# Attention's heads in pairs, and the division by the softmax's sums inside the turn (blocks of weights times diagonals of reciprocal sums)

## What is computed

```python
k = rope(kv[:, :, 0], pos); v = kv[:, :, 1]
q = rope((rmsnorm(x, w['attn_norm']) @ w['w_q']).reshape(b, t, 16, 64), pos)
# swa_prompt: blocks of 128 queries, keys of their own and the previous block
s = jnp.einsum('bnqkgd,bnskd->bnkgqs', qb, kb) * 64 ** -0.5
s = jnp.where(mask, s, -jnp.inf)
m = jnp.maximum(jnp.max(s, axis=-1, keepdims=True), sink)
p = jnp.exp(s - m)
p = p / (jnp.sum(p, axis=-1, keepdims=True) + jnp.exp(sink - m))
o = jnp.einsum('bnkgqs,bnskd->bqkgd', p, vb)
x = x + o @ w['w_o']
```

## Time and profile before

| | |
|---|---|
| median of 3 runs | 3170.84 us (3169.39 to 3171.84) |
| the profiled execution, its own time | 3175.33 us |
| its span in the profile | 3173.5 us |
| PE busy | 3063.0 us (97%) |
| DVE busy | 2544.1 us (80%) |
| mean granted TensorE clock | 0.979 |

### The profile page before, as it was taken

The page is one execution under the profiler, slowest core; times in us unless marked ns, Lnnn a source line. Parts: engine busy times, 40 slices in busy tenths (PEclk is TensorE's granted clock), DMA queues, the critical chain, the costliest instruction groups (busy, mean ns, idle before and its releaser), DMA issues.

```text
span 3173.5 us, 50434 instructions
## 1 busy us (share of the span) xinstructions
PE 3063.0 (97%) x19070; PEld 2973.1 (94%) x19070; DVE 2544.1 (80%) x4947; ACT 1379.8 (43%) x2558; POOL 1882.1 (59%) x1165
## 2 busy tenths in 40 slices
PE   8889999999999999999988899999999999999998
PEld 7779999999999999999875789999999999999998
DVE  7755999977776899989567448999877759998997
ACT  2522344477774333333344233343677753333333
POOL 4543488887776665664130233788877766565651
PEclk9999999999999999999987899999999999999999
DMA  3212499999999999999130022899999999999994
GB/s 111 73 54 92 139 335 347 325 403 393 394 386 367 401 401 398 400 395 398 58 99 1 27 67 85 283 348 347 355 400 394 387 360 398 401 398 400 400 397 191
DMA packets 286337, 920.89 MB, mean 290 GB/s; under 512 B 27344, under 2 KB 77136, under 8 KB 282432
## 3 DMA queue, kind: packets, MB, share of 16 engines
q1 hardware_dynamic: 154080, 415.37, 35.9%
q0 software_dynamic: 111280, 404.77, 33.3%
q10 hardware_dynamic: 20736, 97.53, 7.6%
HBM read 817.07 MB, written 102.38 MB: 290 GB/s over the span
## 4 chain that ended last, share of the span: by engine, by line
PE 67%; DVE 21%; DMA 8%; issue 2%; POOL 1%; ACT 1%; SPq 1%; DVEq 0%; ACTq 0%
PE ps L1767 24%; PE ps L1709 15%; PE ps L1632 10%; PE ps L1712 7%; DMA sring<-s_dram 6%; PE ps L1743 5%; DVE xrest L1168 2%; DVE xl L975 1%; DVE xn L982 1%; DMA gt<-gate_dram 1%; DVE low L1336 1%; DVE cand L1251 1%; DVE cand L1258 1%; DVE rowsB L1161 1%; PE ps L1893 1%
## 5 line engine op out<-in xcount | busy, mean ns | idle before, releaser
L787 ACT ACTIVATE high<-raw 128x1024 fp32r<-128x1024 f32 x512 | 542.8, 1060 | 937.2 <-PE ps L1767 640.2
L629 POOL TENSOR_TENSOR low<-raw,high 128x1024 fp32r<-128x1024 f32 x256 | 614.8, 2402 | 157.6 <-ACT high L787 154.2
L1709 PE MATMUL ps<-xh,high 128*128 128x384 f32 x2048 | 701.4, 342 | 6.3 <-ACT sring L840 6.3
L1767 PE MATMUL ps<-hh,high 128*128 128x384 f32 (+1 forms) x2048 | 691.4, 338 | 7.6 <-DVE low L1336 7.4
L1767 PE MATMUL ps<-hl,high 128*128 128x384 f32 x2048 | 691.7, 338 | 0.0
L1767 PE MATMUL ps<-hh,low 128*128 128x384 f32 x2048 | 690.7, 337 | 0.0
L1709 PE MATMUL ps<-xl,high 128*128 128x384 f32 x2048 | 688.6, 336 | 0.0
L620 POOL DMA_INDIRECT rowsB<-v,pick x192 | 330.0, 1719 | 207.1 <-DVE xrest L1168 192.3
L620 POOL DMA_INDIRECT rowsA<-v,pick x192 | 315.1, 1641 | 213.8 <-DVE xrest L1168 206.5
L1712 PE MATMUL ps<-xh,low 128*128 128x384 f32 x2048 | 399.5, 336 | 7.2 <-POOL low L629 7.2
L1767 PEld LDWEIGHTS ps<-hh,high 128*128 128x128 f32 x2048 | 385.2, 188 | 11.6 <-DVE low L1336 11.4
(11 more groups left out here) (282 smaller groups left out, 5205.3 us busy)
## 6 DMA issues: line engine op xcount, KB each, us to landing
raw<-uT SPq DMA_DIRECT2D x256, 512.0 KB, 6.8
raw<-v SPq DMA_DIRECT2D x256, 512.0 KB, 14.0
gate_dram<-gblk ACTq DMA_DIRECT2D x24, 2048.0 KB, 11.6
s_dram<-sring ACTq DMA_DIRECT2D x120, 384.0 KB, 6.8
gt<-gate_dram SPq DMA_DIRECT2D x30, 1536.0 KB, 20.9
sring<-s_dram SPq DMA_DIRECT2D x120, 384.0 KB, 14.7
raw<-wts SPq DMA_DIRECT2D x74, 512.0 KB, 3.3
rowsB<-u,pick POOLq DMA_INDIRECT x192, 8.0
```

Of the source, the lines that this page charges most:

```text
L629: pool.tensor_tensor(low[:, m % 4], raw[:, m % 4], high[:, (m + 2) % 3].bitcast(F32), ALU.subtract).then_inc(sem("lo_ready"), 1)
L787: act.activation(high[:, (m + 2) % 3], tile_raw(m), ACT.Copy).then_inc(sem("hi_ready"), 1)
L1709: pe.matmul(ps[:, m % 2, 0:DN], a[:, c], x[:, c, 0:DN], start=(c == 0 and k == 0), stop=False)
L1767: ins = pe.matmul(ps[:, c, 0:cols], w[:, c], h[:, n % 3, 0:cols], start=opens, stop=(n == KEYS - 1 and j == 2))
```

## The change

Heads are kept in pairs: `qR` has 128 partitions and 8 slots, a tile of the projection as it is, and `kR` holds each key head twice, in the lower and in the upper 64 partitions. Scores of the even head use rows 0 to 63 of the array and those of the odd head rows 64 to 127; they go to different banks. Mix writes even heads to PSUM partitions 0 to 63 and odd heads to 64 to 127, in twice as many matmuls of half the columns, and keep is one copy of 128 partitions. The division is no longer done on `pr`: DVE multiplies the identity by the reciprocal sums of the four heads (`diag`, 128 x 512), and the turn is a full fp32 matmul of a block of `pr` with a diagonal in place of a transpose. The order of heads in a unit's small arrays becomes even heads first, hence `pairs` and the rearranged sinks. The copy of the sample queries (`qS`) is made in two halves and stands behind the first two units' scale_max. PE's wait for all rotated tiles at the start becomes a wait for the tiles that a unit needs.

```diff
-        qR = st.take("qR", [HD, NH, T])
-        kR = st.take("kR", [HD, NKV, T])
+        qR = st.take("qR", [P, NC, T])
+        kR = st.take("kR", [P, NKV, T])
+        diag = st.take("diag", [P, 2, GRP, P])
@@ rope
-                    chain.did(dve.tensor_tensor(dst[:, 2 * f], rc[0:HD, r], rot[0:HD, r], ALU.add))
-                    ins = dve.tensor_tensor(dst[:, 2 * f + 1], rc[HD:P, r], rot[HD:P, r], ALU.add)
+                    if d0 == D_K:
+                        for e in range(2):
+                            rows = slice(e * HD, (e + 1) * HD)
+                            for at in range(2):
+                                ins = dve.tensor_tensor(kR[at * HD:(at + 1) * HD, 2 * f + e], rc[rows, r], rot[rows, r],
+                                                        ALU.add)
+                                if (e, at) != (1, 1):
+                                    chain.did(ins)
+                    else:
+                        ins = dve.tensor_tensor(qR[:, f], rc[:, r], rot[:, r], ALU.add)
@@ attention, DVE
-                dve.wait_ge(sem("roped"), 2 + NC)
-                dve.tensor_copy(qS[:, :, :, :], qR[:, :, TP:T].rearrange("p h (b s) -> p b h s", b=NB)
-                                ).then_inc(sem("qS_ready"), 1)
@@ normalise
-                    dve.tensor_tensor(p, p, m[:, 5, 0:GRP].unsqueeze(2).broadcast_to([P, GRP, 2 * WIN]),
+                    if u >= 2:
+                        dve.wait_ge(sem("pturn"), u - 1)
+                    dve.tensor_tensor(diag[:, u % 2], ident.unsqueeze(1).broadcast_to([P, GRP, P]),
+                                      m[:, 5, 0:GRP].unsqueeze(2).broadcast_to([P, GRP, P]),
                                       ALU.mult).then_inc(sem("p_ready"), 1)
@@ keep
-                    for e in range(2):
-                        ins = dve.tensor_copy(
-                            ob[e * HD:(e + 1) * HD, 2 * kv:2 * kv + 2, n * WIN:(n + 1) * WIN],
-                            ps[0:HD, OUT, :].rearrange("p (g e q) -> p g e q", g=2, e=2)[:, :, e])
+                    dve.tensor_copy(ob[:, 2 * kv:2 * kv + 2, n * WIN:(n + 1) * WIN],
+                                    ps[:, OUT, 0:2 * WIN].rearrange("p (g q) -> p g q", g=2)
+                                    ).then_inc(sem("o_copied"), 1)
@@ behind the first two scale_max
+                dve.wait_ge(sem("roped"), 2 + NC)
+                by_half = qS[:, :, :, :].rearrange("p b (f e) s -> p b f e s", e=2)
+                for e in range(2):
+                    ins = dve.tensor_copy(by_half[:, :, :, e], qR[e * HD:(e + 1) * HD, :, TP:T]
+                                          .rearrange("p f (b s) -> p b f s", b=NB))
@@ scores, PE
-                pe.wait_ge(sem("roped"), 2 + NC)
-                    for g in range(GRP):
-                        ins = pe.matmul(sbank(k)[:, g // 2, (g % 2) * 256 + lo:(g % 2 + 1) * 256],
-                                        qR[:, kv * GRP + g, n * WIN:(n + 1) * WIN],
-                                        kR[:, kv, ks:(n + 1) * WIN], start=True, stop=True)
+                    if u < NKV:
+                        pe.wait_ge(sem("roped"), 2 + (NC - 1 if u < NKV - 1 else NC))
+                    for g in range(2):
+                        for e in range(2):
+                            ins = pe.matmul(sbank(k)[:, e, g * 256 + lo:(g + 1) * 256],
+                                            qR[e * HD:(e + 1) * HD, 2 * kv + g, n * WIN:(n + 1) * WIN],
+                                            kR[e * HD:(e + 1) * HD, kv, ks:(n + 1) * WIN], start=True, stop=True)
@@ turn
-                            ins = pe.transpose(ps[:, 2 + kb, g * P:(g + 1) * P],
-                                               pr[:, u % PRS, g, kb * WIN:(kb + 1) * WIN], ident)
+                            ins = pe.matmul(ps[:, 2 + kb, g * P:(g + 1) * P],
+                                            pr[:, u % PRS, g, kb * WIN:(kb + 1) * WIN], diag[:, u % 2, g],
+                                            start=True, stop=True)
@@ mix
-                        ins = pe.matmul(ps[0:HD, OUT, :], vtok[:, n - 1 + kb, kv * HD:(kv + 1) * HD],
-                                        prT[:, u % 2, 4 * kb:4 * kb + 4].rearrange("p g q -> p (g q)"),
-                                        start=(kb == kbs[0]), stop=(kb == 1))
+                        for e in range(2):
+                            j = 4 * kb + 2 * e
+                            ins = pe.matmul(ps[e * HD:(e + 1) * HD, OUT, 0:2 * WIN],
+                                            vtok[:, n - 1 + kb, kv * HD:(kv + 1) * HD],
+                                            prT[:, u % 2, j:j + 2].rearrange("p g q -> p (g q)"),
+                                            start=(kb == kbs[0]), stop=(kb == 1))
```

More of the change, by code:

```diff
@@ L524, in _ @@
             spq.wait_ge(sem("k_ready"), 2)
-            spq.dma_start(kNew, kR[:, :, TP - WIN:T]).then_inc(sem("out_done"), 16)
+            spq.dma_start(kNew, kR[0:HD, :, TP - WIN:T]).then_inc(sem("out_done"), 16)
             load_weights(W_Q + 2, W_O + 2)
@@ L1400, in experts, with rope @@
                 dve.memset(mark[:, :], 0.0).then_inc(sem("x_ready"), 1)
-            def rope(d0, n, dst):
+            def rope(d0, n):
                 for f in range(n):
@@ L1419, in attention @@
                 norm_apply(N_KV, X_KV)
-                rope(D_K, 2, kR)
+                rope(D_K, 2)
                 dve.wait_ge(sem("roped"), 2)
@@ L1426, in attention @@
                 norm_apply(N_AT, X_AT, inv=rinv[:, :])
-                rope(D_Q, NC, qR)
-                dve.wait_ge(sem("roped"), 2 + NC)
-                dve.tensor_copy(qS[:, :, :, :], qR[:, :, TP:T].rearrange("p h (b s) -> p b h s", b=NB)
-                                ).then_inc(sem("qS_ready"), 1)
+                rope(D_Q, NC)
                 ob = xn
@@ L1451, in scale_max, with pairs @@
                     chain.settle()
-                    sk = prm[:, P_SINK + kv * GRP:P_SINK + (kv + 1) * GRP]
-                    chain.did(dve.tensor_tensor(m[:, 0, 0:GRP], m[:, 0, 0:GRP], sk, ALU.max))
+                    sk = prm[:, P_SINK + kv * GRP:P_SINK + (kv + 1) * GRP].rearrange("p (g e) -> p e g", e=2)
+                    def pairs(i):
+                        return m[:, i, 0:GRP].rearrange("p (e g) -> p e g", e=2)
+                    chain.did(dve.tensor_tensor(pairs(0), pairs(0), sk, ALU.max))
                     chain.settle()
@@ L1456, in scale_max @@
                     chain.settle()
-                    dve.tensor_tensor(m[:, 3, 0:GRP], sk, m[:, 0, 0:GRP], ALU.subtract
-                                      ).then_inc(sem("pmax"), 1)
+                    dve.tensor_tensor(pairs(3), sk, pairs(0), ALU.subtract).then_inc(sem("pmax"), 1)
                 def normalise(u):
-                    p, m = pr[:, u % PRS], sm[:, u % PRS]
+                    m = sm[:, u % PRS]
                     dve.wait_ge(sem("pexp"), u + 1)
@@ L1472, in keep @@
                     dve.wait_ge(sem("p_out"), u + 1)
-                    for e in range(2):
-                        ins = dve.tensor_copy(
-                            ob[e * HD:(e + 1) * HD, 2 * kv:2 * kv + 2, n * WIN:(n + 1) * WIN],
-                            ps[0:HD, OUT, :].rearrange("p (g e q) -> p g e q", g=2, e=2)[:, :, e])
-                        if e == 0:
-                            chain.did(ins)
-                    ins.then_inc(sem("o_copied"), 1)
+                    dve.tensor_copy(ob[:, 2 * kv:2 * kv + 2, n * WIN:(n + 1) * WIN],
+                                    ps[:, OUT, 0:2 * WIN].rearrange("p (g q) -> p g q", g=2)
+                                    ).then_inc(sem("o_copied"), 1)
                 def sample_scale(k, h):
@@ L1534, in attention @@
                     item(k)
+                dve.wait_ge(sem("roped"), 2 + NC)
[3 more added lines that the diff above has]
+                                          .rearrange("p f (b s) -> p b f s", b=NB))
+                    if e == 0:
+                        chain.did(ins)
+                ins.then_inc(sem("qS_ready"), 1)
                 for u in range(UNITS):
@@ L1860, in sample_scores @@
                             pe.matmul(o[:, 0:WIN], q, kc_sb[:, b, kv], start=True, stop=True)
-                            ins = pe.matmul(o[:, WIN:], q, kR[:, kv, TP + b * TS:TP + (b + 1) * TS],
+                            ins = pe.matmul(o[:, WIN:], q, kR[0:HD, kv, TP + b * TS:TP + (b + 1) * TS],
                                             start=True, stop=True)
```

## The result

The changed kernel takes 3138.28 us (median of 4 runs, 3135.36 to 3144.23), the one before 3171.34 us beside it (3169.39 to 3178.40). The ratio is 0.9894, with a 95% interval of 0.9873 to 0.9915: 33 us, 1.1%, faster. The forecast was 3148, that is 23 us off the median before. Against those the gain is 27 to 29 us.

A forecast was written before the change was run, and what follows sets the result against it. PE bounds the whole kernel; in this stage DVE's work plus its waits for PE do. DVE's 84.0 us plus waits of 8.1, 11.6, 2 and 5.1 gave 110.8, 27 saved from 3175.3: 3148 us, range 3138 to 3163.

The forecast's parts named there:

- step with a sample piece: PE in units 8 to 15: turn, mix, sample piece and scores together fall from 6.49 to 5.7 us.
- row pairs apart: Rival on PE's scores: row pairs don't overlap, costing 13 us, total 3161 us; chance 12%.
- neither pair overlapping: Rival on PE's mix and scores: switching between full and split array use drains it, total 3179 us; chance 5%.
- a turn at the price of four transposes: Rival on PE's turn: 2.2 us more in 15 steps, total 3181 us; chance 3%.
- DVE's wait for mix: Sign in the units' stage, ahead of keep: the wait should fall from 23.2 us to under 12.
- DVE without waits for PE: DVE's own work in the stage: 98.9 us, less 15.7 saved, plus 0.8 for the sample queries' copies, gives 84.0.
- Waits for PE: DVE's waits in the stage: 8.1 us PE-bound steps, 11.6 slow turns, about 2 late start, 5.1 at the end.
- Slow turns: Half-clock turn and mix, at the first turn and behind three samples' pauses: four at 2.9 us, 11.6 in all.
- PE-bound steps and the pause in unit 12: Units 8 to 15: seven steps, 8.1 us over DVE's; PE's late start behind the samples' copies, about 2 us.
- The end: Behind the last normalise: turn, mix, sample piece and last mix, less the cover of one keep, 5.1 us.
- turn and mix just fit: Units 0 to 7: turn, mix and two handovers fit beside scale_max's 3.0 us, costing nothing at full clock.
- the clock never falls once the units run: Rival on PE's clock in the units' stage: 11.6 us more are won, total 3137 us; chance 7%.

The follow-up runs named there:

- e7: The changed kernel with mix unpaired, one matmul of 512 columns a key block, and keep as two copies: 3150.70 us, ratio 0.9941 to the kernel before.
- e8: The changed kernel with all four heads' scores on rows 0 to 63, so its output is not the reference's: 3154.06 us, ratio 0.9951 to the kernel before.
- e9_change: The changed kernel itself, run again unaltered in a later series: 3138.26 us, ratio 0.9913 to the kernel before.
- e3_scores_in_row: The changed kernel with a unit's four scores ordered even, even, odd, odd: 3138.24 us, ratio 0.9919 to the kernel before.
- e6_warm_less: The changed kernel with 2, 3 and 3 extra 512-column matmuls into an unused bank ahead of turns 0, 3 and 5: 3134.43 us, ratio 0.9899 to the kernel before.

## Why the forecast was right in direction and too small

**The mechanism stood.** The terms of PE: turn 1.98 (forecast 1.9), mix 0.92 (0.95), scores 1.06 (1.05), step with a sample piece 5.74 (5.7). Those of DVE: `diag` 0.69 (0.69), one copy 0.42 (0.42), `qS` 0.86 (0.8), start 2.7 to 3.1 us earlier (3.0). Row pairs, for which I had no row, overlap as column strips do: the step with the weakest ground held. Three rivals are settled (row pairs apart, neither pair overlapping, a turn at the price of four transposes): e7 and e8 show what unpaired takes, and the turn took 1.94 times the transposes, at half clock 3.7 us against 1.9. Of the signs that the prediction named, one didn't come: DVE's wait for mix fell to 14.6 us and not under 12, mainly because of the end of the stage (below). The Trainium skill (page "TensorE: Matmul & The Clock Gate", section "Terms") has the transpose mode as four times faster for FP32; no run here shows a factor of four.

**The stage.** Forecast 116.8 us (1641.8 to 1758.6), measured 112.9. DVE without waits for PE: 84.0 forecast; 1753.9 - 1646.9 - 24.6 = 82.4 measured. Waits for PE: 26.8 forecast, 24.6 measured, but with other parts. The term of the sum that was mis-sized most is the first:

- Slow turns: 11.6 forecast (four at 2.9). There were three, none behind the samples' copies, and DVE waited 0.8, 1.95 + 0.3 and 2.8 us behind them, 5.9 in all:

```profile
1678.54 0.42 DVE L1483 COPY xn<-ps 128x256 f32<-128x256 f32 x1 [1.95 <-PE ps L1912]
...
1693.42 0.42 DVE L1483 COPY xn<-ps 128x256 f32<-128x256 f32 x1 [2.80 <-PE ps L1912]
```

- PE-bound steps and the pause in unit 12: 10.1 forecast. DVE's waits there are 1.3 four times and 1.9 once, 7.2. I had counted seven steps at 5.7; the last two have no scores left and take 4.68.

```profile
1712.31 1.23 DVE L1449 SCALAR_TENSOR_TENSOR pr<-ps,atc 128x1024 f32<-128x1024 f32 x1 [1.31 <-PE ps L1863]
```

- The end: 5.1 forecast, 3.25 + 3.24 + 2.27 = 8.8 measured (the rows of the end above), since without scores DVE has nothing to do in those two steps. Some 2.9 us of small waits stand in units 2 to 8, where the prediction had turn and mix just fit and put nothing.

**The step that failed** is the one from the sum to the number: "since part of my gain is clock, I don't take the 27 off the median (3144) but keep 3148". It took the 27.2 us off one execution of 3175.33 us, which lay 4.5 us over the median of three, and 8.6 over that of the 53 later runs. Its guess at the reason holds over the whole span: that execution's mean granted clock was 0.979, and of the 53 runs the four at 0.979 or less averaged 3175 us, the twelve at 0.983 3166.9. But most of the excess was not in this stage. What lies ahead of the first matmul of the values, and what lies behind the mark, is the same in all these kernels but for addresses. In the trace of before these parts take 1566.8 and 1387.6 us; in the 13 other traces 1557.5 to 1567.9 (mean 1563.2) and 1380.7 to 1388.4 (mean 1385.1). So some 6 us of excess stand outside the stage, and about 2.5 of the 8.6 are left for it; both are estimates, from one trace of the kernel before. How far such code varies, by the per-line view of two of the kernels (e9_change, e3_scores_in_row):

```profile
L1848 PE MATMUL ps<-wv_sb,xn x80: 378/379/430, 1561.2 to 1578.4; 128*128 128x256 f32 x64, 128*64 128x256 f32 x16
```

```profile
L1848 PE MATMUL ps<-wv_sb,xn x80: 378/379/430, 1557.5 to 1574.6; 128*128 128x256 f32 x64, 128*64 128x256 f32 x16
```

Taking 27.2 off the median would have given 3143.6, and the stage's measured 31.2 gives 3139.6; the median says 3138.3. Of the 9.7 us that I missed, 4.5 are this step, 4 the stage, and the rest lies within the runs' spread. Part of the 4 may be the same thing again: off the later median of 3166.8 the 27.2 give 3139.6, 1.3 over what was measured. The rival "the clock never falls once the units run" came nearest in its number, 3137, though not in its reason, which makes that luck: the clock did fall three times, and each fall cost less.

**What the change is made of.** The pairs and what comes with them (one copy for keep, the start) carry it all; the start's share was not run by itself and is read from the traces. The other half, the diagonals, gives nothing alone (ratio 1.0006). Beside the pairs it costs the stage 4.7 us without the filling (112.9 against 108.3) and 2.2 with it (109.4 against 107.2), one trace each; the totals (0.9894 and 0.9913 against 0.9906) can't show a difference. I had priced both sides of it nearly right, 0.54 us off DVE and 0.88 onto PE (0.96 measured), but summed the change as one and never asked what each half was worth; the sum of PE's step (5.7 against DVE's 4.53) already said that in units 8 to 12 the second half buys time on the engine that waits.

What stays open: how the 14.6 us divide between mix and the second copy of keep, and what decides whether a slow stretch follows unit 12. Even and odd heads' scores in the same bank were not tried.

## What to carry to other kernels

Where two matmuls use half the array each, in rows or in columns, put them on different halves: here PE then took 0.92 us in place of 1.77 and 1.06 in place of 1.92, and in both orders of the calls that were tried. Before work is moved from one engine to another, look in each stage which of the two waits, and cost each half of a change for itself. And take a forecast made from one profiled execution off as a difference from the median; its distance to the median belongs to the whole span unless a stage can be shown to hold it. A median of three or four runs moves too: that of the kernel before lay between 3163.8 and 3171.3 us in five series.

## What was not expected of the hardware

- PE takes matmuls of the other half of the array past several records that stand ahead of them in program order: even, even, odd, odd took 1.14 us for eight records of 256 columns, as even, odd, even, odd did.
- Row halves (64 of 128 rows) overlap nearly as fully as column halves: 1.92 to 1.06 us for scores, 1.77 to 0.92 for mix.
- A full fp32 matmul in place of a fp32 transpose takes 1.94 times as long (1.98 against 1.02 us for eight), and 1.96 times at half clock (3.72 against 1.90).
- Three matmuls of 512 columns (2.84 us) put into a pause of about 4 us (in e6_warm_less, ahead of turn 3 and of turn 5) left the clock at 1.00 through it; without them it read 0.50 behind the pause.
